# Scores of the first units made inside the last projection job in three of the attention layers

## The reference, cut to what matters

```python
def odd_mixer(h, w_qkv, q_norm, k_norm, rel_table, w_out):
    q, k, v = jnp.split(h @ w_qkv, 3, axis=-1)
    q = rms_norm_2(split_heads(q, N_HEADS_CHUNK), q_norm)
    k = rms_norm_2(split_heads(k, N_HEADS_CHUNK), k_norm)
    o = chunk_band_attention(q, k, split_heads(v, N_HEADS_CHUNK), rel_table)
    return merge_heads(o) @ w_out
```

## Time and profile before

| | us |
|---|---|
| median of 3 runs | 2000.18 |
| the profiled execution | 1999.24 |
| its span, first to last instruction | 1997.5 |
| TensorE busy | 1933.7 (97%) |
| VectorE busy | 1522.3 (76%) |
| ScalarE busy | 1272.0 (64%) |
| first attention, start of its scores | 152.8 |
| fourth | 606.0 |
| sixth | 1744.4 |

### The profile page before, as it was taken

The page is one execution under the profiler, slowest core; times in us unless marked ns, Lnnn a source line. Parts: engine busy times, 40 slices in busy tenths (PEclk is TensorE's granted clock), DMA queues, the critical chain, the costliest instruction groups (busy, mean ns, idle before and its releaser), DMA issues.

```text
span 1997.5 us, 26032 instructions
## 1 busy us (share of the span) xinstructions
PE 1933.7 (97%) x9572; PEld 1592.1 (80%) x9572; DVE 1522.3 (76%) x1718; ACT 1272.0 (64%) x1400; POOL 96.2 (5%) x102
## 2 busy tenths in 40 slices
PE   6999999999998999999999999999999989999998
PEld 4887887888887788888888888888888867778876
DVE  7666766544586789989898988989989884467686
ACT  4544676534545677777787777877777765446464
POOL 1000300000000320000000000000000000100001
PEclk9999999999999999999999999999999999999999
DMA  9863645555452599999999999999999995624500
GB/s 366 275 226 120 213 169 191 203 183 189 159 193 82 180 412 367 377 387 365 385 356 392 370 381 376 373 388 358 380 387 370 377 366 169 211 64 149 174 1 32
DMA packets 186269, 535.14 MB, mean 268 GB/s; under 512 B 12609, under 2 KB 23893, under 8 KB 186198
## 3 DMA queue, kind: packets, MB, share of 16 engines
q1 hardware_dynamic: 179952, 518.95, 71.0%
q10 hardware_dynamic: 4422, 8.92, 1.2%
q0 software_dynamic: 1824, 6.31, 1.1%
HBM read 521.02 MB, written 13.12 MB: 267 GB/s over the span
## 4 chain that ended last, share of the span: by engine, by line
PE 85%; DVE 7%; ACT 4%; DMA 2%; issue 2%; ACTq 0%; DVEq 0%; SPq 0%
PE bank L467 25%; PE bank L469 24%; PE bank L468 24%; DVE WL L1193 3%; ACT WH L1189 2%; PE bank L671 1%; DMA ring<-in_od_we_down 1%; PE bank L660 1%; PE bank L2772 1%; DVE P L1177 1%; PE bank L375 1%; PE bank L439 1%; PE bank L686 1%; PE bank L684 1%; DMA ring<-in_od_we_up 1%
## 5 line engine op out<-in xcount | busy, mean ns | idle before, releaser
L1193 DVE TENSOR_TENSOR WL<-ring,WH 128x2048 fp32r<-128x2048 f32 x475 | 1073.0, 2279 | 257.6 <-ACT WH L1189 254.0
L1189 ACT ACTIVATE WH<-ring 128x2048 fp32r<-128x2048 f32 x475 | 901.8, 1912 | 351.0 <-PE bank L469 332.0
L467 PE MATMUL bank<-WH,XTH 128*128 128x512 f32 (+1 forms) x1872 | 738.3, 394 | 9.2 <-DVE XTL L396 3.0
L469 PE MATMUL bank<-WH,XTL 128*128 128x512 f32 (+1 forms) x1872 | 727.8, 389 | 0.0
L468 PE MATMUL bank<-WL,XTH 128*128 128x512 f32 (+1 forms) x1872 | 727.1, 388 | 0.0
L467 PEld LDWEIGHTS bank<-WH,XTH 128*128 128x128 f32 x1872 | 352.6, 188 | 95.0 <-DVE WL L1193 14.7
L469 PEld LDWEIGHTS bank<-WH,XTL 128*128 128x128 f32 x1872 | 352.5, 188 | 73.5
L468 PEld LDWEIGHTS bank<-WL,XTH 128*128 128x128 f32 x1872 | 353.0, 189 | 68.8 <-issue 0.2
L467 PE MATMUL bank<-WH,HTH 128*128 128x512 f32 (+1 forms) x568 | 219.9, 387 | 1.4 <-DVE WL L1193 1.1
L469 PE MATMUL bank<-WH,HTL 128*128 128x512 f32 (+1 forms) x568 | 217.9, 384 | 0.0
L468 PE MATMUL bank<-WL,HTH 128*128 128x512 f32 (+1 forms) x568 | 217.6, 383 | 0.0
(11 more groups left out here) (450 smaller groups left out, 1382.2 us busy)
## 6 DMA issues: line engine op xcount, KB each, us to landing
ring<-in_od_we_gate SPq DMA_DIRECT2D x112, 1024.0 KB, 7.2
ring<-in_od_we_up SPq DMA_DIRECT2D x112, 1024.0 KB, 8.5
ring<-in_od_we_down SPq DMA_DIRECT2D x112, 1024.0 KB, 8.4
ring<-in_w_in SPq DMA_DIRECT2D x20, 1024.0 KB, 6.8
ring<-in_fox_w_in SPq DMA_DIRECT2D x16, 1024.0 KB, 6.6
ring<-in_nsa_w_in SPq DMA_DIRECT2D x14, 1024.0 KB, 5.0
ring<-in_w_ada SPq DMA_DIRECT2D x12, 1024.0 KB, 10.3
ring<-in_ev_w_in SPq DMA_DIRECT2D x12, 1024.0 KB, 5.2
```

The lines of the kernel that those rows point to most:

```text
L467: nc.tensor.matmul(out, x[0], wt[0][:, k, :], start=start, stop=False, skip_group_check=check)
L469: return nc.tensor.matmul(out, x[1], wt[0][:, k, :], start=False, stop=stop, skip_group_check=check)
L1189: nc.scalar.activation(wh, slot_ap(n, nk, width), ACT.Copy).then_inc(hi_made, 1)
L1193: nc.vector.tensor_tensor(wl, slot_ap(n, nk, width), wh.bitcast(F32), ALU.subtract).then_inc(lo_made, 1)
```

## The change

- `Project` gets `shift`, which rotates the pair of banks of its jobs; P1 has `shift=1`, so that its job 9 is in banks 0 and 1 and job 8 in 2 and 3.
- First attention: TensorE makes the scores of pairs 0 and 1 in the hook (9, 1, 0), between the two parts of job 9. ScalarE's exponentials of units 0 to 3 are in `during[9]`, ahead of the eviction of job 9. VectorE's four maxima follow `P1.dve`, ahead of `P1.wait`. `A1.pe` begins with the turns of pair 0 and waits for P1's last eviction after the scores of pair 2.
- Sixth attention: the same with job 8 of P6.
- Fourth attention: the query transposes go to the hook (4, 1) of P4, the key transposes to (5, 0, 1), the scores of pair 0 to (5, 1, 0). VectorE copies the turned queries ahead of the keys' norm, in `during[4]`. The exponentials of units 0 and 1 are in `during[5]`. `P4.wait` comes after the turns of pair 0, ahead of the scores of pair 1.
- `Attention` gets parameters for this (`entered`, `ended`, `soon`, `turned_pairs`, `first`, `end`), and the waits on `roped` behind the fourth stage count one more.

```diff
--- before.py
+++ after.py
@@ -472,15 +472,15 @@
-            def __init__(self, jobs, lhs, scale=None, narrow=None, tall=None, by_parts=0):
-                self.jobs, self.lhs, self.scale, self.by_parts = jobs, lhs, scale, by_parts
+            def __init__(self, jobs, lhs, scale=None, narrow=None, tall=None, by_parts=0, shift=0):
+                self.jobs, self.lhs, self.scale, self.by_parts, self.shift = jobs, lhs, scale, by_parts, shift
                 self.narrow, self.tall = narrow, tall
                 self.ba = base["proj_act"]
                 base["proj_act"] += len(jobs)
             def out(self, c, tt):
-                return bank[4 + tt if c == 2 and self.by_parts == 3 else (2 * c + tt) % 4]
+                return bank[4 + tt if c == 2 and self.by_parts == 3 else (2 * (c + self.shift) + tt) % 4]
             def pe(self, pe, operand, beside={}, late=None):
@@ -686,23 +686,28 @@
                 nc.tensor.matmul(bank[g % 2 * 2 + 1][:, o], p[:, 256:384], v(0), start=False, stop=True,
                                  skip_group_check=True).then_inc(valued, 1)
-            def pe(self, pe, early=None, first=0):
+            def pe(self, pe, early=None, first=0, entered=None, ended=None, soon=0, turned_pairs=0):
                 N = len(self.units) // 2
                 for p in range(N + 2):
+                    if entered and p == 1:
+                        entered()
                     if first <= p < N:
                         self.scores(pe, p)
+                    if ended and p == 2:
+                        ended()
                     for a in range(2):
-                        if 1 <= p <= N:
+                        if 1 + turned_pairs <= p <= N:
                             self.turn(pe, 2 * (p - 1) + a)
                         if p >= 2:
                             self.weigh(pe, 2 * (p - 2) + a)
-                        if early and (p, a) in ((N, 1), (N + 1, 0)):
-                            if p == N:
+                        step = 2 * (p - N) + a - 1 + soon
+                        if early and step in (0, 1):
+                            if step == 0:
                                 pe.wait_ge(maxed, self.u + 2 * N)
-                            early(1 - a)
-
-            def act(self, act):
-                for i in range(len(self.units)):
+                            early(step)
+
+            def act(self, act, first=0, end=None):
+                for i in range(first, len(self.units) if end is None else end):
                     g, uu = i // self.G, i % self.G
                     act.wait_ge(maxed, self.u + i + 1)
                     if uu == 0 and g >= 2:
@@ -734,7 +739,7 @@
                     dve.wait_ge(valued, self.u + j - 1)
                 nc.vector.tensor_copy(PT[j % 2], bank[6 + j % 2][:, 0:384]).then_inc(copied, 1)
-            def dve(self, dve, early=None, gate=None):
+            def dve(self, dve, early=None, gate=None, first=0):
                 N, G = len(self.units) // 2, self.G
                 due = {}
                 for g in range(len(self.units) // G):
@@ -744,7 +749,7 @@
                         due[p + 1] = (g, (1,))
                 for p in range(N + 3):
                     for a in range(2):
-                        if p < N:
+                        if first <= p < N:
                             self.highest(dve, 2 * p + a)
                     if gate and p == N:
                         gate()
@@ -813,7 +818,7 @@
         gate_ready, gate_ps, gate_set = sem("gate_ready"), sem("gate_ps"), sem("gate_set")
         T1 = Transposes([(lambda tt, k=k: XN[:, tt, k * 128:k * 128 + 128], xt_dest(k), None) for k in range(KD)], split=True)
         P1 = Project([(c_in1[i], 512, pcol(in1_order[i], 512), {512: ACT.Silu, 2560: ACT.Silu}.get(in1_order[i], ACT.Copy)
-                       if in1_order[i] < 3072 else ACT.Sigmoid) for i in range(10)], xt, by_parts=3)
+                       if in1_order[i] < 3072 else ACT.Sigmoid) for i in range(10)], xt, by_parts=3, shift=1)
         TQ1 = HeadTransposes(query_pairs(1024, 4, 0, -0.125), key_pairs(1536, 4, 0))
         d_made, d_copied, y_made, y_gated = sem("d_made"), sem("d_copied"), sem("y_made"), sem("y_gated")
@@ -1697,8 +1702,8 @@
             act.dma_start(ADA_GATE[0:1, :], t["b_ada"][:, 2 * D:3 * D]).then_inc(gate_bias, 16)
             act.dma_start(BAND, t["band"]).then_inc(band_in, 16)
             act.dma_start(GRP, t["w_pool_grp"][0].rearrange("g c d -> c g d")).then_inc(band_in, 16)
-            P1.act(act, {3: lambda: TQ1.act(act)})
-            A1.act(act)
+            P1.act(act, {3: lambda: TQ1.act(act)}, {9: lambda: A1.act(act, 0, 4)})
+            A1.act(act, 4)
             TY1.act(act)
             TA1.act(act)
             act.dma_start(GAIN, t["g_final"].partition_broadcast(128)).then_inc(gfin_in, 16)
@@ -1819,11 +1824,14 @@
             norm_act(act, 2, T4)
             roots(act, stat[:, 0:2])
             scaled(act, "act_root")
-            P4.act(act, {2: lambda: roots(act, stat[:, 16:48]), 4: lambda: roots(act, stat[:, 16:48])})
-            TQ4.act(act)
-            act.wait_ge(rw_in, 16)
-            nc.scalar.activation(RH, RW[:, :, :], ACT.Copy).then_inc(r_hi, 1)
-            A4.act(act)
+            def keys4():
+                TQ4.act(act, 4)
+                act.wait_ge(rw_in, 16)
+                nc.scalar.activation(RH, RW[:, :, :], ACT.Copy).then_inc(r_hi, 1)
+
+            P4.act(act, {2: lambda: roots(act, stat[:, 16:48]), 4: keys4},
+                   {4: lambda: (roots(act, stat[:, 16:48]), TQ4.act(act, 0, 4)), 5: lambda: A4.act(act, 0, 2)})
+            A4.act(act, 2)
             TO4[0].act(act)
             split_until(act, c_out3[2][0] + 1)
             TO4[1].act(act)
@@ -1885,8 +1893,8 @@
                 nc.scalar.activation(FA, FA, ACT.Ln, bias=1.0).then_inc(f_ln, 1)
             P6.act(act, {2: forget, 4: lambda: TQ6.act(act, 0, 4), 5: lambda: TQ6.act(act, 4)},
-                   {2: lambda: P6.narrow_act(act, 1)})
-            A6.act(act)
+                   {2: lambda: P6.narrow_act(act, 1), 8: lambda: A6.act(act, 0, 4)})
+            A6.act(act, 4)
             TO6[0].act(act)
             split_until(act, c_out4[2][0] + 1)
             TO6[1].act(act)
@@ -2040,8 +2048,10 @@
             P1.dve(dve, {0: lambda: rope(dve, P[:, :, 1024:1536], cos0, sin0, 8, TT), 1: keys1,
                          3: lambda: TQ1.dve(dve), 5: pooled, 6: angles, 7: pool_gated})
             dve.sem_inc(gate_ready, 1)
+            for i in range(4):
+                A1.highest(dve, i)
             P1.wait(dve)
-            A1.dve(dve, lambda: TY1.dve(dve))
+            A1.dve(dve, lambda: TY1.dve(dve), first=2)
             A1.wait(dve)
             last = nc.vector.tensor_tensor(O[:, :, 0:512], O[:, :, 0:512], P[:, :, 2560:3072], ALU.mult)
@@ -2167,15 +2177,20 @@
             rms(dve)
-            P4.dve(dve, {1: lambda: head_sums(dve, 0), 2: lambda: head_norm(dve, 0, [(0, 16, "od_q")]),
-                         3: lambda: head_sums(dve, 1024), 4: lambda: head_norm(dve, 1024, [(0, 16, "od_k")])})
-            dve.sem_inc(roped, 1)
-            P4.wait(dve)
-            TQ4.dve(dve)
+            def heads4(c0, name):
+                head_norm(dve, c0, [(0, 16, name)])
+                dve.sem_inc(roped, 1)
+
+            P4.dve(dve, {1: lambda: head_sums(dve, 0), 2: lambda: heads4(0, "od_q"), 3: lambda: head_sums(dve, 1024),
+                         4: lambda: TQ4.dve(dve, 4)},
+                   {4: lambda: (TQ4.dve(dve, 0, 4), heads4(1024, "od_k"))})
             dve.wait_ge(r_hi, 1)
             nc.vector.tensor_tensor(RL, RW[:, :, :], RH.bitcast(F32), ALU.subtract).then_inc(r_lo, 1)
             dve.wait_ge(r_lo, 1)
-            A4.dve(dve, lambda: TO4[0].dve(dve))
+            for i in range(2):
+                A4.highest(dve, i)
+            P4.wait(dve)
+            A4.dve(dve, lambda: TO4[0].dve(dve), first=1)
             A4.wait(dve)
             nc.vector.memset(stat[:, 60:61], 0.0).then_inc(p_free, 1)
@@ -2326,8 +2341,10 @@
                 TQ6.dve(dve, 0, 4)
             P6.dve(dve, {1: forget_in, 2: forget, 4: forget_sums, 5: lambda: TQ6.dve(dve, 4)})
+            for i in range(4):
+                A6.highest(dve, i)
             P6.wait(dve)
-            A6.dve(dve, lambda: TO6[0].dve(dve), lambda: gate6(dve))
+            A6.dve(dve, lambda: TO6[0].dve(dve), lambda: gate6(dve), 2)
             A6.wait(dve)
             gate_half(dve, g6, 1)
             split_until(dve, c_out4[2][0] + 1)
@@ -2560,11 +2577,17 @@
                                                 stop=True, skip_group_check=True)
                 last.then_inc(y_made, 1)
-            P1.pe(pe, T1, {2: other_columns, (2, 0, 1): last_columns, 4: heads1, 6: differences, 8: mixed_groups})
-            P1.wait(pe)
-            TQ1.wait(pe)
+            def first_scores1():
+                TQ1.wait(pe)
+                pe.wait_ge(d_copied, 1)
+                A1.scores(pe, 0)
```

(47 more changed lines are left out.)

## The result

| | before | after |
|---|---|---|
| median, us | 2000.95 (11 executions, 1999.63 to 2003.99) | 2010.12 (11 executions, 2001.34 to 2016.29) |
| ratio | | 1.0042, 95% interval 1.0028 to 1.0057 |
| the profiled execution | 1999.24, span 1997.5 | 2001.34, span 1999.6 |
| its mean granted TensorE clock | 0.996 | 0.994 |
| TensorE busy | 1933.7 | 1936.2 |

The kernel became slower by 9 us, where 1.8 less were forecast. The time lies above the range's end of 2001.2, and beyond the 0.2% that can be told from no change.

The account below looks back on a forecast made before the run. TensorE, busy 97% of the span, bounds the kernel; only gaps at three seams can be won. First -0.7, fourth +0.4, sixth -1.5 sum to -1.8 us: median 2000.18 goes to 1998.4, range 1995.4 to 2001.2.

Parts of the forecast that it names:

- TensorE's gaps at the seams as the only place: Between last projection matmul and first full loop turn of three attentions: only these gaps can be won, 8.8 us together.
- ScalarE's order: First and sixth attention: exponentials stand ahead of the last projection job's eviction, with a table load between them.
- The load's price: ScalarE's table switch: the load takes 1.28 us and the next activation starts 0.01 later.
- the rival of dearer switches: Evictions at the seams: a switch holds ScalarE another 1.28 us beyond its load; +0.8, 2001.0 us; 14 in 100.
- the drain: ScalarE's table switches: the skill page adds about 1380 ns, 2.66 us per switch; the sum would be +1.0.
- No reload: First and sixth evictions: gate functions use the exponentials' table, so the loads ahead vanish; 1996.1 us; 10 in 100.
- The keys' wait: Fourth projection's last job: TensorE waits about 1.9 us for the keys' norm, behind VectorE's queue.
- The fourth's third unit: Fourth attention: the third unit's transposes start at 611.4 instead of 611.00, 0.4 us lost.
- The second load is covered: First attention: the load back to exponentials delays nothing; unit 4 is ready with 0.7 us to spare.
- VectorE's wait: First and sixth seams: third unit starts when the eviction ends, 157.1 and 1748.7, winning 0.7 and 1.5 us.
- what costs nothing: Bank shift, later WL chunk halves and their loads, GpSimd's queue and renumbered counts: no wait added, no order changed.
- a gap on TensorE of some 2.2: First attention, expected sign in the profile: gap before the third unit's turn, released by the last projection eviction.

Follow-up runs that it names:

- early copies: Only the first attention changed against the kernel before, with VectorE's wait for P1's last eviction moved behind its first two copies; median 2005.44 us.

## Why the prediction was wrong

**What held.** *TensorE's gaps at the seams as the only place* where time can be won: yes; the loss lies behind them. *ScalarE's order* at the first and the sixth, exponentials, load, eviction, load: the load at 154.57 and the eviction at 155.86 stand within 0.2 us of the sum. *The load's price*: 1.28, and the eviction starts 0.01 behind it, for Sigmoid (154.57 to 155.86) as for Silu; so the rival of dearer switches falls, and with it the drain that the page of the Trainium skill adds (ScalarE: Activation LUTs, What ACT_TABLE_LOAD costs), which no row here shows. *No reload* falls by the same rows. *The keys' wait*: 1.69 by VectorE's queue, 1.9 forecast. *The fourth's third unit*: 0.5 later, 0.4 forecast. *The second load is covered*: unit 4 follows without a gap of TensorE.

**First failed step: VectorE's wait.** The prediction let the third unit start when the eviction had ended ("turn(2) starts at 157.1", "1748.7"). TensorE's own wait indeed opens there, but `turn(2)` also needs unit 0's copy, and VectorE stands at `P1.wait(dve)`, ahead of its copies, until the same eviction. So a copy of 0.56 and its hand-over come on top: 0.7 at the first seam, where the gain of 0.7 becomes 0.0, and 0.7 at the sixth, where 1.5 becomes 0.8. I had listed what is queued behind the wait on TensorE and ScalarE, and not what is behind it on VectorE. The early copies showed the size, 0.68. With this alone the forecast would have been 1999.9.

**Second failed step: the gap's effect on the clock.** It isn't a term of the wrong size but one that was not there. Under "what costs nothing" banks, queues and loads were looked at; the clock was taken as 1.00. The text itself forecast "a gap on TensorE of some 2.2", in one piece, where the earlier trace rows have 1.18, 1.25 and 0.33 with work between. By the sum of idle time that is a gain. By the clock it is a loss of about 7 us: filling the gap gives it back. A page of the Trainium skill (TensorE: Matmul & The Clock Gate, Why this matters for your kernels) warns of idle gaps between bursts of matmuls, since the clock gate then goes back to half rate. The traces agree that it does (0.50 behind the wait of 2.99), but not on how long a gap it takes: the page's figure would have let the forecast gap of 2.2 pass, and here the clock fell behind waits of 2.30 and 1.56. Still, the rule names a rival, "the clock falls behind the merged gap", that was missing from the list. Part of its price is plain, since each microsecond at half clock costs half a microsecond; how many there would be (6.8 to 17.1 in the traces of the merged gap) stood in no row of before.

**Third: the range.** It was built from waits of ±0.5 us and had no case in which work outside the gaps runs slower. Its upper end, 2001.2, is less than one short stretch at half clock away. The spread of the runs before (2000.02 to 2001.02, three of them) hid that single executions of the same kernel reach 2018: three runs are too few to see an event that hits one in five.

## What to carry to other kernels

Add up idle time, but look at how it is cut as well: three short waits with work between (1.18, 1.25 and 0.33 us) cost TensorE its clock in three traces of six, for 3.4 us each; one wait of 2.3 to 3.6 us cost it in five of five, for 6.8 to 17.1 us. Where an engine whose clock can fall must wait, idle products in the gap can be worth more than a shorter gap. When a wait is moved, list what stands behind it on every engine that has it, not only on the one that is watched. When the executions of a changed kernel spread more than before, put the granted clock beside each time before looking for a longer path, and look in each trace for the place where the clock fell: it may be one that the edit doesn't touch.

## What the runs showed of the hardware

Behind the same wait (2.99 and 2.98 us) TensorE ran at half clock for 6.8, 13.7 and 17.1 us in three executions. It did so while it was busy without a gap (17.00 of 17.00 us), so more work doesn't bring the clock back at once. Behind the waits of 2.3 us or more at this seam the low clock began 0 to 1.3 us after the wait had ended, so the first transposes can still run at full speed (0.52 us at 157.68). The length of a wait doesn't settle what follows: behind the one of 2.37 at 1638 us, in every kernel, the clock fell in 5 of 19 traces and for 3.4 us; behind 1.56 at the fourth seam it fell in one for 10.2 us; behind 1.8 at the sixth in none of three. It is a matter of chances: with longest waits of 2.98, 2.30, 2.07, 1.55 and 0.60 us at the first seam, 11, 8, 8, 6 and 1 of 12 executions were above 2003 us, where falls at other places are counted too.
